# One reciprocal for two units: pairing the softmax normalisation in the attentions of a two-model kernel

## What is computed

```python
def forgetting_attention(q, k, v, f_pre, gq, gk):        # first model, 4 heads of 128
    s = jnp.einsum('bqhd,bkhd->bhqk', qi, k) + (Fi[..., :, None] - Fk[:, :, None, :])
    s = jnp.where(pos_k[None, :] <= pos_q[:, None], s, -jnp.inf)
    p = jax.nn.softmax(s, axis=-1)
    return jnp.einsum('bhqk,bkhd->bqhd', p, v)
...
def hybrid_mixer(...):                                   # second model, 4 heads of 64 in each mixer
    y_a = mla_mixer(...)             # a causal softmax attention
    y_b = nsa_mixer(...)             # o = g0 * o_cmp + g1 * o_slc + g2 * o_win: three softmax attentions, gated
    y_c = dsa_mixer(...)             # softmax over the 128 best keys by an index score
    y_d = stick_breaking_mixer(...)  # no softmax
```

## Time and profile before

| | us |
|---|---|
| median of 3 runs | 3440.46 (3432.53 to 3441.02) |
| the profiled execution's own time | 3431.76 |
| its span, first to last instruction | 3430.0 |
| TensorE busy over the span | 3276.2 |
| VectorE busy | 1550.5 |
| ScalarE busy | 1289.9 |
| the two large phases (64 units each) | about 92 each |
| the two small phases (16 units each) | about 23 each |
| the first model's attention (16 units) | about 40 |

### The profile page before, as it was taken

The page is one execution under the profiler, slowest core; times in us unless marked ns, Lnnn a source line. Parts: engine busy times, 40 slices in busy tenths (PEclk is TensorE's granted clock), DMA queues, the critical chain, the costliest instruction groups (busy, mean ns, idle before and its releaser), DMA issues. The chain is left out here.

```text
span 3430.0 us, 37430 instructions
## 1 busy us (share of the span) xinstructions
PE 3276.2 (96%) x14880; PEld 2630.2 (77%) x14880; DVE 1550.5 (45%) x2443; ACT 1289.9 (38%) x2234; POOL 331.2 (10%) x156
## 2 busy tenths in 40 slices
PE   7999999999999999999889999999999988899998
PEld 6867678878888888877666788878887767678886
DVE  4154522244343333446975433443334488663333
ACT  3344642333232322234665422242223446642222
POOL 0411324400000000014000000000000330000000
PEclk9999999999999999999999999999999999999999
DMA  4311223323333333322001233323332310023332
GB/s 145 92 43 44 86 62 105 99 80 101 96 99 98 98 94 98 98 99 90 13 1 62 86 99 98 94 85 98 97 94 101 105 50 1 19 80 98 97 94 74
DMA packets 77069, 280.60 MB, mean 82 GB/s; under 512 B 8800, under 2 KB 9056, under 8 KB 76640
## 3 DMA queue, kind: packets, MB, share of 16 engines
q1 hardware_dynamic: 76896, 278.21, 25.9%
HBM read 276.08 MB, written 2.10 MB: 81 GB/s over the span
## 5 line engine op out<-in xcount | busy, mean ns | idle before, releaser
L539 ACT ACTIVATE w_hi<-raw_slabs 128x1024 fp32r<-128x1024 f32 x496 | 524.5, 1058 | 1285.4 <-PE ps L579 1132.6
L554 DVE TENSOR_TENSOR w_lo<-raw_slabs,w_hi 128x1024 fp32r<-128x1024 f32 x372 | 454.9, 1223 | 747.7 <-ACT w_hi L539 747.5
L579 PE MATMUL ps<-in_hi,w_hi 128*128 128x512 f32 x1840 | 719.8, 391 | 9.6 <-DVE in_lo L902 7.7
L579 PE MATMUL ps<-in_lo,w_hi 128*128 128x512 f32 x1840 | 717.4, 390 | 0.0
L579 PE MATMUL ps<-in_hi,w_lo 128*128 128x512 f32 x1840 | 717.3, 390 | 0.0
L579 PE MATMUL ps<-parts,w_hi 128*128 128x512 f32 x2240 | 691.5, 390 | 0.9 <-DVE scratch L1480 0.8
L554 POOL TENSOR_TENSOR w_lo<-raw_slabs,w_hi 128x1024 fp32r<-128x1024 f32 x124 | 307.1, 2479 | 2472.9 <-ACT w_hi L539 2472.9
L579 PEld LDWEIGHTS ps<-parts,w_hi 128*128 128x128 f32 x2240 | 420.3, 188 | 90.8 <-issue 1.9
L579 PE MATMUL ps<-parts,w_lo 128*128 128x512 f32 x1120 | 435.8, 389 | 0.0
L579 PEld LDWEIGHTS ps<-in_hi,w_hi 128*128 128x128 f32 x1840 | 346.1, 188 | 87.3 <-issue 8.7
L579 PEld LDWEIGHTS ps<-in_hi,w_lo 128*128 128x128 f32 x1840 | 346.4, 188 | 72.4
(11 more groups left out here) (277 smaller groups left out, 3491.7 us busy)
## 6 DMA issues: line engine op xcount, KB each, us to landing
raw_slabs<-weights SPq DMA_DIRECT2D x510, 512.0 KB, 3.6
big<-rope SPq DMA_DIRECT2D x2, 2304.0 KB, 8.9
x_resid<-xT SPq DMA_DIRECT2D x8, 256.0 KB, 4.6
outT<-x_resid SPq DMA_DIRECT2D x8, 256.0 KB, 2.0
const_cols<-consts SPq DMA_DIRECT2D x1, 836.0 KB, 9.1
scratch<-brow SPq DMA_DIRECT2D x1, 768.0 KB, 9.9
vector_cols<-vec SPq DMA_DIRECT2D x2, 45.5 KB, 9.6
vector_cols<-vec SPq DMA_DIRECT2D x1, 69.0 KB, 3.3
```

Source lines behind the costliest of these rows:

```text
L539: self.nc.scalar.activation(self.w_hi[:, m % SPLIT, :], self.raw[:, n % RAW, :], ACT.Copy)\
L554: (self.nc.gpsimd if i is None else self.nc.vector).tensor_tensor(self.w_lo[:, m % SPLIT, :], self.raw[:, n % RAW, :], self.w_hi[:, m % SP ...
L579: mm = k.nc.tensor.matmul(out, lhsT, rhs, start=(c == 0 and m == 0), stop=(last and m == 2))
```

## The change

VectorE no longer takes a reciprocal in every step. In odd steps (and step 0) it does the row maximum and the top step alone. In every even step i from 2 on, after the row maximum and the top step, it takes the reciprocals of units i-2 and i-1 in one instruction on 128x2, and then normalises unit i-2 and unit i-1. The signal `row_inv` counts pairs. Nothing else is edited, on no other engine.

```diff
@@ attention_phase
+    assert n % 2 == STATS % 2 == 0
...
                 take_top(k, dve, index, share(steps, i, n + 1), steps.start)
-                if i >= 1:
-                    u = units[i - 1]
-                    p = probs(i - 1)[:, 0:u.width]
-                    inv = col(1, i - 1)
-                    dve.wait_ge(expd, k.at(expd, i))
-                    nc.vector.reciprocal(inv, inv).then_inc(row_inv, 1)
-                    dve.wait_ge(row_inv, k.at(row_inv, i))
+                if i == 0 or i % 2:
+                    continue
+                at = (i - 2) % STATS
+                pair = k.stat[:, 1, at:at + 2]
+                dve.wait_ge(expd, k.at(expd, i))
+                nc.vector.reciprocal(pair, pair).then_inc(row_inv, 1)
+                dve.wait_ge(row_inv, k.at(row_inv, i // 2))
+                for m in (i - 2, i - 1):
+                    u, p, inv = units[m], probs(m)[:, 0:units[m].width], col(1, m)
                     if u.gate is not None:
                         nc.vector.tensor_scalar(p, p, inv, u.gate, ALU.mult, ALU.mult).then_inc(probs_ready, 1)
...
-    k.passed(..., row_inv=n, probs_ready=n,
+    k.passed(..., row_inv=n // 2, probs_ready=n,
```

More of the change, by code:

```diff
@@ L1954, in _ @@
                 lay_and_store(k, act, i - lag, n, units, turned, laid, unit_done, stored)
-    k.passed(scored=n, row_max=n, bias_scaled=scaled[-1], probs_expd=n, row_inv=n, probs_ready=n,
+    k.passed(scored=n, row_max=n, bias_scaled=scaled[-1], probs_expd=n, row_inv=n // 2, probs_ready=n,
              turned=n, laid=n, unit_done=n, stored=groups, top8=len(steps), top8_taken=len(steps),
```

## The result

| | before | changed |
|---|---|---|
| median of 5 runs | 3440.28 us (3432.53 to 3441.02) | 3454.30 us (3453.12 to 3467.27) |
| profiled execution, own time | 3431.76 | 3454.30 |
| its span | 3430.0 | 3452.5 |
| VectorE busy | 1550.5 | 1539.1 |

The ratio of the changed kernel to the kernel before is 1.006, with a 95% interval of 1.0046 to 1.0074: the change makes the kernel slower by 0.5 to 0.7%. VectorE has less work (11 us less). By the medians the kernel takes 14 us more, by the means of the five runs each (3438.6 and 3458.5) 20 us, and by the two profiles 22.5 us. One of the 12 runs of a later experiment, the one with all top steps in odd steps, took 6689.09 us at a mean granted clock of 0.523; it stands in no ratio.

The account below looks back on a forecast made before the run. The loop between VectorE and TensorE in the large phases was taken to bound the change: +15 us there and +2 elsewhere, +17 on the runs' middle, 3436, gave 3453 us. The range was 3437 to 3465.

Parts of the forecast that it names:

- The bound: Whole kernel and large phases: TensorE busy 96% of the span, VectorE 45%; in the large phases both nearly full, of 92.3 us.
- The loop: Large phases: turn, weigh, score, maximum, any top step, reciprocal, normalisation form a closed loop, once per pair of units.
- The walk: Large phase, 16 units traced through the queues from row maximum R(18): R(34) at 24.3 us, where the trace before has 21.97.
- the term was 7.5 each: Large phases: four patterns lose 1.9 + 2.3 + 1.8 + 1.5 = 7.5 us in each phase, 15 us in both.
- The signs: Changed profile: large phases 98 to 101 us, VectorE busy about 81, TensorE about 82, more idle ahead of turns and row maxima.
- the lower bound: Price of the unseen 128x2 reciprocal: 0.15 us, no dearer than 128x1; the upper bound was 0.29 us.
- a pure VectorE bound: Large phases: if VectorE alone set the pace, 32 fewer reciprocals of 0.19 us in each would give 12.2 us.
- The other phases: First model's attention and small phases: steady part costs nothing; three later ends and the small phases' starts together cost 2 us.
- The thin cover: Small phase, steady part: TensorE reaches an even unit's turn at least 0.15 us after its normalisation is ready, so no cost.
- the last rival: Large phases: gaps on TensorE make the clock fall, up to 10 us more, 3463 us; chance 0.06.
- the first: Whole kernel: slower because the moved normalisations delay the loop, +17 us (10 to 25); chance 0.70.
- The rule on grouping: Large phases: by the skill's rule for a saturated engine, 64 removed reciprocals should gain 12 us; the prediction said lose 15.

## Why the prediction was right

**The bound.** Reading the stages and not the average was what mattered. TensorE is busy 95% of the changed span and VectorE 45%, hardly other than in rows 1, and the kernel is slower.

**The loop.** The walk foretold the places. From R(18), in us:

| | walk | changed trace |
|---|---|---|
| R(20) | 3.32 | 1684.90 - 1681.57 = 3.33 |
| N(18) | 4.79 | 4.76 |
| turn(18) | 5.19 | 5.16 |
| R(22) | 6.40 | 6.43 |
| R(34) | 24.3 | 1705.91 - 1681.57 = 24.34 |

The other patterns came out above it: R(2) to R(18) 24.6 (walk 23.7), R(34) to R(50) 25.6 (25.1), R(50) to the last products 27.7 (27.4). So the large phases cost 9.3 and 9.2 us more, where the term was 7.5 each: sized a fifth too low. The first pattern's 0.9 us fit the clock: the walk used durations at full speed, and the changed phase runs its first 10.7 us at the lower level (0.50), the kernel before only its first 4.0 (0.50). The run with the top steps in odd steps shows a price of that with identical instructions, in its first and its second layer from R(2) to R(18):

```profile
1661.28:1685.65 24.37, 23.08 (x133) 19.03 (x133) 19.50 (x61) 14.36 (x55) 0.00 (x0) 0.78 0.00 1
2823.84:2846.99 23.15, 21.33 (x133) 17.37 (x133) 19.31 (x62) 14.35 (x55) 0.00 (x0) 0.88 0.00 1
```

1.2 us for 0.10 of clock, that is for 5.4 us more at the lower level. In other kernels the price is lower: between the two layers of the paired kernel with later turns 6.7 us more at the lower level go with 0.7 us of M, and with the top step last as well 6.7 us more go with nothing (90.1 in both). The half us of the third pattern stays unexplained; the walk is rounded at every step.

**The signs.** VectorE's idle time grew as named, and TensorE's waits for the normalisation ahead of the turns grew from 4.8 us (both kinds of normalisation) to 14.8. A large phase takes 101.5 and 101.4 us, just above the 98 to 101 that was named, and TensorE is busy 86.1 us in it and not about 82: more of it ran at the lower clock.

**The reciprocal.** 128x2 takes 156 ns in the first large phase (157 over the span), and 128x1 took 153 there (154): the lower bound was right to take. Its slot (1686.14 to 1686.33) is 0.19 us as before. The 12.2 us that I gave as the gain of a pure VectorE bound were too high: without any move half of that shows in M.

**The other phases.** 0.85 us in each small phase and 0.5 in the first model's attention are 2.2 us, the term was 2. The thin cover in the small phase's steady part held.

**The clock.** The profile's 22.5 us hold 3 us at the stick phases' ends that no step of the prediction had; they are the clock's, not the queue's. In each large phase, too, some 7 us more ran at the lower level (0.95, from 0.98), which by the prices above is nothing to 1.5 us a phase, an estimate. So the last rival was at work beside the first, at no more than some 6 us of its 10, and not instead of it.

**The median.** The median of 3454.3 was foretold at 3453; that two so near numbers meet is partly luck. The profile is 5 us above its sum (3454.3 against 3449), and the median of before, 3440.28, lies 4 above the middle that I took. In the runs beside the experiments the kernel before has medians of 3433 to 3435; against those the change costs about 20 us, where 17 were foretold.

**The rule on grouping.** The Trainium skill (Perfetto Trace Analysis, Optimizing Scalar/DVE Operations) ties its advice to a saturated engine. VectorE at 93% looked like one; the run with half of the reciprocals left out shows it to be half of one: M fell by 3.0 of 6.1 us. Grouping made the group wait for its last member and for what stands ahead of it, and a large phase came out 9.3 us longer, three times what the saving alone gives back. The prediction also cited the section's other advice, to break instructions up where they cause bubbles elsewhere, without its condition, that the engine isn't saturated. The two kernels bear it out with the condition, read from the changed one back to the one before: VectorE is busy 81.9 of 101.5 us, TensorE stands 14.8 us for it, and with the pairs broken up a large phase is 9.3 us shorter. What counts is the place: breaking up the reciprocal alone, where it stands, made M 2 us longer.

## What to carry to other kernels

Before you merge two small instructions, look at what the first of the two results releases. If the merged one stands later in its queue, count the loop: from that result through the other engines back to this queue, with everything that stands ahead of it now. In the paired kernel, where VectorE and TensorE wait for each other, the independent top steps were dear ahead of the result that TensorE waits for (98 us) and cheap away from there (90 to 92), until TensorE got one more step of slack. In the kernel before their place was worth 0.3 us only: there the waits for ScalarE grew as those for the normalisation fell.

Read a change's effect in the phases first: here a phase lost 9 us of 92, and its tenths were plain in one profile, where most of the whole runs of one kernel spread over some 10 us.

## What the runs showed of the hardware

The spread of the runs of one kernel has a place. The first model's attention, with TensorE recorded busy without a break, takes 32.1 us at a granted clock of 1.00 in the profile of before, 40.1 at 0.79 with the same instructions on TensorE, and 44.0 at 0.69 in a kernel with later turns, which at 1.00 takes 31.3 (with pairing, where the same stretch ran at the upper level throughout). From the first to the last row maximum, in the kernel before, in the one with the top step last and single reciprocals, and in the one with later turns and single reciprocals:

```profile
259.90:292.00 32.10, 32.10 (x151) 18.48 (x152) 16.20 (x60) 15.73 (x53) 0.00 (x0) 1.00 0.01 3
```

```profile
261.10:301.20 40.10, 40.10 (x151) 23.20 (x151) 16.20 (x61) 15.74 (x53) 0.00 (x0) 0.79 0.01 1
```

```profile
259.40:303.40 44.00, 44.00 (x143) 24.53 (x144) 16.24 (x60) 15.08 (x51) 0.00 (x0) 0.69 0.00 1
```

These are two levels, 2.4 and 1.2 GHz, in different parts; in the second execution the lower one lay over 17.1 us and in the third over 27.3. In the 25 us ahead of the fall TensorE stood still nowhere for more than 0.43 us, as in the kernel before, and within these stretches the busy share in the records was 100%, so a busy TensorE in the profile is no sign that the clock is granted. Where TensorE sets the pace, as here, a microsecond at the lower level cost just under half of one (8.0 us for 17.1, 12.7 for 27.3); in the large phases it cost nothing to 0.22.

The runs of the kernel before beside the experiments fall into two bunches, with four in between: those up to 3433.5 us have a mean clock of 0.986 to 0.988, those from 3437 us on one of 0.981 to 0.986. That this phase is what tells the two apart in unprofiled runs is not shown; a fall of the clock in it was seen in four profiled ones, those at 3441 to 3450 us.
